# One of four channel blocks of a depthwise convolution goes from VectorE to GpSimd

## The chip, the cores and the metric

The kernel runs on one core of a Trainium2 chip, as one launch in float32. The metric is the device time of one execution in microseconds, the median of several runs. A core has TensorE (matmul, weight load), VectorE (elementwise and reductions), ScalarE (activation functions), GpSimd (elementwise, and DMAs with computed addresses) and SyncE (here only DMAs). They run side by side and wait for each other through semaphores. In the profile they are PE (and PEld), DVE, ACT, POOL and SP.

## The reference: what is computed

It is one inference step of a decoder layer for a prompt group of 1024 tokens and a sample group of 8. Three branches (latent attention, a convolution module, cross-attention to a memory) are gated, added, projected, and followed by a mixture of experts. The change lies in the convolution module. Its input is the gated product of 512 channels; `hist` puts 30 zero rows (prompt) or 30 state rows (sample) ahead of it. Each channel has its own 31 taps:

```python
y = lax.conv_general_dilated(hist, w_dw[:, None, :], window_strides=(1,), padding='VALID',
                             dimension_numbers=('NWC', 'WIO', 'NWC'), feature_group_count=C_CONV)
y = jax.nn.silu(layer_norm(y + b_dw, g_ln, b_ln))
return y @ w_conv_out
```

The layer norm is over the 512 channels, so its mean needs all of them. The merge is `(g_a * y_mla + g_b * y_conv + g_c * y_mem) @ w_out`.

## The kernel before, in words

The kernel is a chain of stages with a barrier between them: constants, front, tokens, sample, merge, mixer, experts. The change is in `stage_merge` alone, which runs from about 1121 to 1597 us of the profile. All engines' programs are written out by hand, each in a fixed order, with semaphores between them.

Channels lie on the partitions: 512 channels are KC = 4 blocks of 128, tokens run along the free dimension (SEQ = 1024, with the sample group TOK = 1032). The stage has three parts of KD = 8 blocks of output channels, a block has three units of 344 tokens, so there are 72 units u. Units 0 to 23 (up to U_C) take the attention branch, 24 to 47 (up to U_B) the memory branch, 48 to 71 the convolution branch.

- TensorE computes for a unit the gate (`pG`, 8 products in k, L1664; not for units 24 to 47, whose gates were stored earlier) and the branch (`pY`, 4 products in k, L1669). `pY` has two buffers: the branch of unit u waits for `unit_used` of u + 2, which is VectorE's merge of unit u - 2, and the gate of unit u for the merge of u - 3. In the profile each product appears as two passes (x8 is one unit's branch, x16 one unit's gate).
- ScalarE takes the sigmoid of the gate (L1561, or L1558 from stored gates). In units 0 to 3 it also takes the sigmoid of one block of convolution gates (L1564).
- VectorE merges the unit: L1617 for the first branch, L1621 and L1623 for the others. In units 0 to 3 it also writes one block of `hist` (L1607) and of `hist_s` (L1608), each marked on the semaphore `glu`.
- Behind the merge, VectorE runs a piece of the prompt's convolution, `conv(first, to)`: NTAP = 4 x 31 = 124 taps in order, four in unit 0, five a unit up to unit 23, three a unit after. A block's first tap is a `tensor_scalar` with the bias (L1593), the others are a `scalar_tensor_tensor` of 128x1024 that adds hist times tap to y (L1596), each waiting for the one before on the semaphore `tap`. After a block's last tap come three short operations for the sample group (L1599, L1601, L1603), marked on `conv_s`.
- In unit 23 VectorE also copies the last rows out of PSUM (L1635, L1636).
- After block b = KD (unit 26) TensorE waits for `conv_s` = 12 and `last_ready`, and adds y over the channels with a matrix of ones: `sums(y, 0)`, L1675 and L1677. The mean is used in units 27 to 30 (L1644), the squares (L1568) are summed after unit 32, the normalised values (L1652, L1576) are TensorE's input from unit 48 on.
- GpSimd clears three buffers and copies the sample group's attention outputs at the stage's start, and has nothing more to do in it.

Of the kernel before, what the change touches and what calls it, by code (L numbers as in the profile page):

```python
# [13 lines left out]
ALU = mybir.AluOpType  # L14
ACT = mybir.ActivationFunctionType
AX = mybir.AxisListType

P = 128
D = 1024
KD = D // P  # L20
SEQ = 1024
NT = SEQ // P
DB = 8
TOK = SEQ + DB
# [5 lines left out]
KC = CC // P  # L30
CW = 31
# [18 lines left out]
def spread(ap, n, at=1):  # L50

    v = ap.unsqueeze(at)
    shape = list(v.shape)
    shape[at] = n
    return v.broadcast_to(shape)
# [1387 lines left out]
def stage_merge(nc, a, o, keep):  # L1443
# [4 lines left out]
    U_C, U_B, U_END = 3 * KD, 6 * KD, 9 * KD  # L1448
    U_LAST, U_MEAN, U_VAR = U_C // 2, U_C + 3, U_C + 9
    PROMPT_END = SEQ - 2 * GN  # L1450
    NTAP = KC * CW
    with Core(nc) as c:
        ring = [c.sb(f"branch_w{r}", [P, 2 * KD, P]) for r in range(W)]
        gates = [ring[r][:, 4:2 * KD, :].rearrange("p k n -> p (k n)")[:, 0:TOK] for r in range(W)]
# [13 lines left out]
        mean = c.sb("ln_mean", [P, TOK])  # L1468
        state = mean[0:120, 0:2 * CC].rearrange("p (g c) -> p g c", g=2)
        ones = c.sb("ones", [P, P])  # L1470
        last = c.sb("last_rows", [HIST, CC])
        last_s = c.sb("last_rows_s", [DB, CC])
        eps = c.sb("eps", [P, 1])
# [3 lines left out]
        pX = c.ps("pSums")  # L1477
        pMs = pX[:, 0:2 * DB]
        S = {n: c.sem("m_" + n) for n in """small_in state_in cleared o_in o_sample unit_psum sig_ready unit_used gated taps_psum taps_ready
            state_psum state_ready glu_sig glu tap conv_s mean_psum mean_ready centred squares var_psum sqrt_ready recip normed conv_ready  # L1480
            last_psum last_ready stored state_moved""".split()}
        w_in = [c.sem(f"m_w_in{r}") for r in range(W)]
        raw_in = [c.sem(f"m_raw_in{i}") for i in range(KC)]
# [4 lines left out]
        with c.block() as block:  # L1488
# [43 lines left out]
            @block.gpsimd  # L1532
            def _(pool):
                pool.memset(ones[:, :], 1.0).then_inc(S["cleared"], 1)
                pool.memset(hist[:, :, 0:HIST], 0.0).then_inc(S["cleared"], 1)
                pool.memset(eps[:, :], EPS).then_inc(S["cleared"], 1)
                pool.tensor_copy(oT[:, 0, :, SEQ:TOK], keep.oT_s[:, :, :]).then_inc(S["o_sample"], 1)
                pool.tensor_copy(oT[:, 1, :, SEQ:TOK], keep.moT_s[:, :, :]).then_inc(S["o_sample"], 1)

            @block.scalar  # L1540
            def _(act):
# [37 lines left out]
            def _(v):  # L1579
# [3 lines left out]
                def conv(first, to):  # L1583

                    for n in range(first, min(to, NTAP)):
                        i, j = divmod(n, CW)
                        if n == 0:
                            v.wait_ge(S["small_in"], 64)
                            v.wait_ge(S["taps_ready"], 1)
                            v.wait_ge(S["state_ready"], 2)  # L1590
                        if j == 0:
                            v.wait_ge(S["glu"], 2 * i + 2)
                            v.tensor_scalar(y[:, i, 0:SEQ], hist[:, i, 0:SEQ], taps[:, i, 0:1], b_dw[:, i:i + 1], ALU.mult, ALU.add).then_inc(S["tap"], 1)  # L1593
                            continue
                        v.wait_ge(S["tap"], n)
                        v.scalar_tensor_tensor(y[:, i, 0:SEQ], hist[:, i, j:j + SEQ], taps[:, i, j:j + 1], y[:, i, 0:SEQ],  # L1596
                                               ALU.mult, ALU.add).then_inc(S["tap"], 1)
                        if j == CW - 1:
                            v.tensor_tensor(prod_s[:, :, :], hist_s[:, i, :, :], spread(taps[:, i, :], DB), ALU.mult).then_inc(S["conv_s"], 1)  # L1599
                            v.wait_ge(S["conv_s"], 3 * i + 1)  # L1600
                            v.tensor_reduce(y[:, i, SEQ:TOK], prod_s[:, :, :], AX.X, ALU.add).then_inc(S["conv_s"], 1)  # L1601
                            v.wait_ge(S["conv_s"], 3 * i + 2)
                            v.tensor_scalar(y[:, i, SEQ:TOK], y[:, i, SEQ:TOK], b_dw[:, i:i + 1], None, ALU.add).then_inc(S["conv_s"], 1)  # L1603

                def gated_unit(i):
                    v.wait_ge(S["glu_sig"], i + 1)
# [19 lines left out]
                for u in range(U_END):  # L1626
                    merge(u)
                    if u < KC:
                        gated_unit(u)
                    step = (4 if u == 0 else 5) if u < U_C else 3  # L1630
                    conv(done, done + step)
                    done += step
                    if u == U_C - 1:
                        v.wait_ge(S["last_psum"], 1)
                        v.tensor_copy(last[:, :], pM[0:HIST, 0:CC]).then_inc(S["last_ready"], 1)  # L1635
                        v.tensor_copy(last_s[:, :], pM[0:DB, CC:2 * CC]).then_inc(S["last_ready"], 1)  # L1636
                    if u == U_MEAN:
                        v.wait_ge(S["mean_psum"], 1)
                        v.tensor_scalar(mean[:, 0:SEQ], pM[:, :], -1.0 / CC, None, ALU.mult)
                        v.tensor_scalar(mean[:, SEQ:TOK], pMs[:, 0:DB], -1.0 / CC, None, ALU.mult).then_inc(S["mean_ready"], 1)  # L1640
                        v.wait_ge(S["mean_ready"], 1)
                    if U_MEAN <= u < U_MEAN + KC:
                        i = u - U_MEAN
                        v.tensor_tensor(y[:, i, :], y[:, i, :], mean[:, :], ALU.add).then_inc(S["centred"], 1)  # L1644
                    if U_VAR + 1 <= u < U_VAR + 4:
                        i = u - U_VAR - 1
                        v.wait_ge(S["sqrt_ready"], 1)
                        v.reciprocal(mean[:, i * GN:(i + 1) * GN], mean[:, i * GN:(i + 1) * GN]).then_inc(S["recip"], 1)
                    if U_VAR + 4 <= u < U_VAR + 4 + KC:
                        i = u - U_VAR - 4  # L1650
                        v.wait_ge(S["recip"], 3)
                        v.tensor_tensor(y[:, i, :], y[:, i, :], mean[:, :], ALU.mult).then_inc(S["normed"], 1)  # L1652

            @block.tensor
            def _(pe):
# [16 lines left out]
                def sums(src, col):  # L1672
                    for at in (0, 512):
                        for i in range(KC):
                            pe.matmul(pM[:, at:at + 512], ones[:, :], src[:, i, at:at + 512], start=i == 0, stop=i == KC - 1)  # L1675
                    for i in range(KC):
                        mm = pe.matmul(pMs[:, col:col + DB], ones[:, :], src[:, i, SEQ:TOK], start=i == 0, stop=i == KC - 1)  # L1677
                    return mm
# [24 lines left out]
                for b in range(KD, 2 * KD):  # L1703
                    block_of(b, oT[:, 1, :, :])
                    if b == KD:
                        pe.wait_ge(S["last_ready"], 2)
                        pe.wait_ge(S["conv_s"], 3 * KC)
                        sums(y, 0).then_inc(S["mean_psum"], 1)
                    if b == KD + 2:
                        pe.wait_ge(S["mean_ready"], 1)  # L1710
                        pe.wait_ge(S["squares"], KC)
                        sums(convT, DB).then_inc(S["var_psum"], 1)
# [714 lines left out]
```

## Time and profile before

| what | value |
| --- | --- |
| median of 3 runs | 3020.0 us (3019.23 to 3020.17) |
| profiled execution, its own time | 3025.34 us |
| span in the profile | 3023.6 us |
| mean granted TensorE clock | 0.949 of full speed |
| TensorE busy | 2775.9 us (92%) |
| VectorE busy | 1083.5 us (36%) |
| ScalarE busy | 621.3 us (21%) |
| GpSimd busy | 863.7 us (29%) |

The profile is of one execution. Its times count from its first instruction; its own time is 5.3 us above the median of the runs, and 1.7 us above its span. Busy shares are means over stages that differ much, so the merge stage has to be read by itself.

### The profile page before, as it was taken

Reading aid. Unit: us, or ns where it says so; the run is one execution under the profiler, and the core shown is the slowest. Engines: PE = TensorE matmul, PEld = TensorE weight load, DVE = VectorE, ACT = ScalarE, POOL = GpSimd, SP = SyncE. Lnnn points to the kernel's source line nnn. Section 1 sums busy time; section 2 is a strip of 40 time slices with the busy share of each in tenths; the row PEclk is TensorE's granted clock in tenths of the full one; section 3 lists DMA queues with packets and bytes.
Section 4 is the critical chain, followed back from the end, with each engine's and each line's share of the span. In section 5 each row is a group of like instructions: output and inputs, shape, how many; then the busy total and the mean of one; then the engine's idle time right before and its main releaser. Section 6 shows DMA issues by size and latency. Waiting matters only on the chain. (4 is left out here: it accounts for less than half of the span.)

```text
span 3023.6 us, 34530 instructions
## 1 busy us (share of the span) xinstructions
PE 2775.9 (92%) x12222; PEld 1854.5 (61%) x12222; DVE 1083.5 (36%) x2253; ACT 621.3 (21%) x1186; POOL 863.7 (29%) x680
## 2 busy tenths in 40 slices
PE   6999999998999976989996998489999999999996
PEld 4566666655555544655663444277777777777774
DVE  3233444453333324995111443322222222222221
ACT  2233333332333311004000110011111111111111
POOL 1000000000544420000000222255555555555552
PEclk9999999997999977989997988789999999999998
DMA  7111110103322114112104111189999999999995
GB/s 252 37 42 47 40 38 26 33 20 84 101 74 81 46 41 141 37 42 75 32 11 159 42 59 39 59 293 303 292 297 295 301 293 298 295 300 294 299 295 147
DMA packets 212823, 428.02 MB, mean 142 GB/s; under 512 B 52898, under 2 KB 134580, under 8 KB 196249
## 3 DMA queue, kind: packets, MB, share of 16 engines
q1 hardware_dynamic: 164592, 316.35, 30.7%
q0 software_dynamic: 35168, 100.78, 13.2%
q10 hardware_dynamic: 12960, 9.58, 1.0%
q8 instruction: 58, 0.95, 0.1%
q14 instruction: 45, 0.36, 0.0%
HBM read 351.23 MB, written 80.68 MB: 143 GB/s over the span
## 5 line engine op out<-in xcount | busy, mean ns | idle before, releaser
L2162 POOL DMA_INDIRECT xg<-tokens_normed,gather_rows x384 | 369.1, 961 | 132.3 <-issue 117.3
L2297 PE MATMUL pGe<-xT,we_g 128*128 128x192 f32 x2048 | 352.7, 331 | 45.1 <-DVE xT L2249 45.1
L2297 PEld LDWEIGHTS pGe<-xT,we_g 128*128 128x128 f32 x2048 | 334.0, 191 | 96.2 <-issue 96.2
L2297 PE MATMUL pUe<-xT,we_u 128*128 128x192 f32 x2048 | 343.3, 326 | 0.0
L2297 PEld LDWEIGHTS pUe<-xT,we_u 128*128 128x128 f32 x2048 | 334.6, 190 | 0.0
L2185 POOL DMA_INDIRECT sums<-yb,add_rows x128 | 195.9, 1531 | 352.4 <-ACT yb L2213 307.2
L1318 PE MATMUL pKs<-ws_uk,cTs 128*128 128x512 f32 x512 | 254.2, 642 | 1.1 <-ACT cTs L1105 1.1
L805 PE MATMUL pFill<-hT,fill_w 128*128 128x344 f32 x768 | 239.5, 456 | 7.1 <-ACT fill_out L514 7.0
L1664 PE MATMUL pGate<-hT,branch_w 128*128 128x344 f32 x768 | 232.1, 455 | 10.9 <-DMA oT<-attention_out 10.9
L1083 POOL TENSOR_TENSOR rk<-ssk,half 128x32 f32<-128x32 f32 x32 | 173.4, 5427 | 216.0 <-DVE ssk L1187 216.0
L2307 PE MATMUL pYe<-we_d,h_e 128*128 128x512 f32 x512 | 230.3, 592 | 0.0
L1664 PEld LDWEIGHTS pGate<-hT,branch_w 128*128 128x128 f32 x768 | 146.9, 191 | 88.0 <-DMA oT<-attention_out 11.3
L2249 DVE STREAM_TRANSPOSE xT<-xg 128x1536 f32<-128x1536 f32 x64 | 189.4, 2959 | 20.5 <-DMA xg<-tokens_normed,gather_rows 20.5
L805 PEld LDWEIGHTS pFill<-hT,fill_w 128*128 128x128 f32 x768 | 141.7, 190 | 83.6 <-issue 21.8
L2255 DVE TENSOR_TENSOR h_e<-silu,pUe 128x384 f32<-128x384 f32 x64 | 35.5, 554 | 435.3 <-PE pUe L2297 435.3
L2213 ACT ACTIVATE yb<-pYe,wc 128x512 f32<-128x512 f32 x128 | 87.9, 687 | 472.1 <-PE pYe L2307 472.1
L1244 DVE TENSOR_REDUCE ssk<-sqs 128x8 f32<-128x512 f32 x128 | 87.6, 684 | 237.8 <-ACT sqs L1131 237.4
L1318 PEld LDWEIGHTS pKs<-ws_uk,cTs 128*128 128x128 f32 x512 | 99.3, 205 | 104.2 <-issue 101.2
L1596 DVE SCALAR_TENSOR_TENSOR y_conv<-hist,taps,y_conv 128x1024 f32<-128x1024 f32 x120 | 154.0, 1284 | 3.4
L2280 DVE TENSOR_SCALAR yb<-pZe,wc 64x512 f32<-64x512 f32 x64 | 47.5, 743 | 300.1 <-PE pZe L2313 300.1
L2307 PEld LDWEIGHTS pYe<-we_d,h_e 128*128 128x128 f32 x512 | 95.5, 190 | 92.7 <-issue 92.7
L2020 PE MATMUL pXf<-w_out,mT 128*128 128x512 f32 x288 | 127.1, 600 | 15.0 <-DMA w_out<-in_w_out 15.0
(387 smaller groups left out, 3201.9 us busy)
## 6 DMA issues: line engine op xcount, KB each, us to landing
we_g<-in_w_e_gate SPq DMA_DIRECT2D x64, 1024.0 KB, 5.2
we_u<-in_w_e_up SPq DMA_DIRECT2D x64, 1024.0 KB, 9.6
we_d<-in_w_e_down SPq DMA_DIRECT2D x64, 1024.0 KB, 14.6
mergedT<-in_cache_latent SPq DMA_DIRECT2D x96, 128.0 KB, 2.1
raw_columns<-fill_out SPq DMA_DIRECT2D x48, 172.0 KB
fill_w<-in_w_in SPq DMA_DIRECT2D x16, 512.0 KB, 4.3
branch_w<-in_w_in SPq DMA_DIRECT2D x16, 512.0 KB, 4.3
xg<-tokens_normed,gather_rows POOLq DMA_INDIRECT x384
```

Source lines behind the costliest of these rows:

```text
L805: mm = pe.matmul(pG[:, 0:GN], ring[b % 2][:, k, :], keep.hT[:, k, g * GN:(g + 1) * GN], start=k == 0, stop=k == KD - 1)
L1083: pool.tensor_tensor(rk[b % 2][:, :, g, :], ssk[b % 2][:, :, g, :], half[:, :].rearrange("p (j h) -> p j h", h=NHEAD), ALU.pow).then_inc(S ...
L1318: mm = pe.matmul(pK[n % 2][:, :], cT[b % 2][:, k, n * P:(n + 1) * P], w_uk[:, k, :], start=k == 0, stop=k == KL - 1)
L1596: v.scalar_tensor_tensor(y[:, i, 0:SEQ], hist[:, i, j:j + SEQ], taps[:, i, j:j + 1], y[:, i, 0:SEQ], ALU.mult, ALU.add).then_inc(S["tap"], 1)
L1664: pe.matmul(pG[g][:, 0:n], ring[r][:, 4 + k, :], keep.hT[:, k, at:at + n], start=k == 0, stop=k == KD - 1)
L2020: mm = pe.matmul(pX[:, half * 512:(half + 1) * 512], mT[:, k, :], w_out[:, k, half * 512:(half + 1) * 512], start=k == 0, stop=k == KD - 1)
L2162: pool.indirect_dma_start(out=xg[s % 2][:, g, :], out_offset=None, in_=quarter, in_offset=bass.IndirectOffsetOnAxis(ap=gi[s][:, g:g + 1], ...
L2185: pool.indirect_dma_start(out=keep.acc_dram[:, :], out_offset=bass.IndirectOffsetOnAxis(ap=si[r][0:n_of[g], g:g + 1], axis=0), in_=yb[r % ...
L2213: act.activation(yb[r % 2][:, 0, half * 512:(half + 1) * 512], pY[half][:, :], ACT.Copy, scale=wc[r][:, 0:1]).then_inc(S["y_act"], 1)
L2249: v.transpose(xT[p][:, :, :].rearrange("p c (g i) -> p g c i", g=NG_E), xg[p][:, :, :].rearrange("p g (j c) -> p g c j", c=KD)).then_inc(S ...
L2297: mm = pe.matmul(dst[r % 2][:, f * CAP:(f + 1) * CAP], w[r][:, k, f * P:(f + 1) * P], xT[r % 2][:, k, :], start=k == 0, stop=k == KD - 1)
L2307: mm = pe.matmul(pY[half][:, :], h[r % 2][:, f, 0:P], wd[r][:, f, half * 512:(half + 1) * 512], start=f == 0, stop=f == 1)
```

## The change

The fourth block of channels (KV = 3) of the prompt's convolution is computed on GpSimd, the first three stay on VectorE. VectorE's NTAP becomes 93, four taps in each of units 0 to 23 (the last has one), none after. GpSimd waits until all four blocks of `hist` are written (`glu` = 8) and runs the first tap with the bias as before; for each of the other 30 taps it writes the product into the new buffer `one_tap` and adds that to y, and each of these waits for the one before (`pool_tap`, `pool_mult`). The sample group's three short operations become a function, `conv_sample(i)`; all four blocks of it stay on VectorE, the fourth in unit 23. TensorE's sums and VectorE's subtraction of the mean also wait for `pool_tap` = 31.

```diff
--- before.py
+++ after.py
@@ -1448,7 +1448,8 @@
     U_C, U_B, U_END = 3 * KD, 6 * KD, 9 * KD
     U_LAST, U_MEAN, U_VAR = U_C // 2, U_C + 3, U_C + 9
     PROMPT_END = SEQ - 2 * GN
-    NTAP = KC * CW
+    KV = KC - 1
+    NTAP = KV * CW
     with Core(nc) as c:
         ring = [c.sb(f"branch_w{r}", [P, 2 * KD, P]) for r in range(W)]
         gates = [ring[r][:, 4:2 * KD, :].rearrange("p k n -> p (k n)")[:, 0:TOK] for r in range(W)]
@@ -1468,6 +1469,7 @@
         mean = c.sb("ln_mean", [P, TOK])
         state = mean[0:120, 0:2 * CC].rearrange("p (g c) -> p g c", g=2)
         ones = c.sb("ones", [P, P])
+        one_tap = c.sb("one_tap", [P, SEQ])
         last = c.sb("last_rows", [HIST, CC])
         last_s = c.sb("last_rows_s", [DB, CC])
         eps = c.sb("eps", [P, 1])
@@ -1477,7 +1479,7 @@
         pX = c.ps("pSums")
         pMs = pX[:, 0:2 * DB]
         S = {n: c.sem("m_" + n) for n in """small_in state_in cleared o_in o_sample unit_psum sig_ready unit_used gated taps_psum taps_ready
-            state_psum state_ready glu_sig glu tap conv_s mean_psum mean_ready centred squares var_psum sqrt_ready recip normed conv_ready
+            state_psum state_ready glu_sig glu tap pool_tap pool_mult conv_s mean_psum mean_ready centred squares var_psum sqrt_ready recip normed conv_ready
             last_psum last_ready stored state_moved""".split()}
         w_in = [c.sem(f"m_w_in{r}") for r in range(W)]
         raw_in = [c.sem(f"m_raw_in{i}") for i in range(KC)]
@@ -1536,6 +1538,16 @@
                 pool.memset(eps[:, :], EPS).then_inc(S["cleared"], 1)
                 pool.tensor_copy(oT[:, 0, :, SEQ:TOK], keep.oT_s[:, :, :]).then_inc(S["o_sample"], 1)
                 pool.tensor_copy(oT[:, 1, :, SEQ:TOK], keep.moT_s[:, :, :]).then_inc(S["o_sample"], 1)
+                pool.wait_ge(S["small_in"], 64)
+                pool.wait_ge(S["taps_ready"], 1)
+                pool.wait_ge(S["glu"], 2 * KC)
+                rows = y[:, KV, 0:SEQ]
+                pool.tensor_scalar(rows, hist[:, KV, 0:SEQ], taps[:, KV, 0:1], b_dw[:, KV:KC], ALU.mult, ALU.add).then_inc(S["pool_tap"], 1)
+                for j in range(1, CW):
+                    pool.wait_ge(S["pool_tap"], j)
+                    pool.tensor_scalar(one_tap[:, :], hist[:, KV, j:j + SEQ], taps[:, KV, j:j + 1], None, ALU.mult).then_inc(S["pool_mult"], 1)
+                    pool.wait_ge(S["pool_mult"], j)
+                    pool.tensor_tensor(rows, rows, one_tap[:, :], ALU.add).then_inc(S["pool_tap"], 1)
 
             @block.scalar
             def _(act):
@@ -1596,11 +1608,16 @@
                         v.scalar_tensor_tensor(y[:, i, 0:SEQ], hist[:, i, j:j + SEQ], taps[:, i, j:j + 1], y[:, i, 0:SEQ],
                                                ALU.mult, ALU.add).then_inc(S["tap"], 1)
                         if j == CW - 1:
-                            v.tensor_tensor(prod_s[:, :, :], hist_s[:, i, :, :], spread(taps[:, i, :], DB), ALU.mult).then_inc(S["conv_s"], 1)
-                            v.wait_ge(S["conv_s"], 3 * i + 1)
-                            v.tensor_reduce(y[:, i, SEQ:TOK], prod_s[:, :, :], AX.X, ALU.add).then_inc(S["conv_s"], 1)
-                            v.wait_ge(S["conv_s"], 3 * i + 2)
-                            v.tensor_scalar(y[:, i, SEQ:TOK], y[:, i, SEQ:TOK], b_dw[:, i:i + 1], None, ALU.add).then_inc(S["conv_s"], 1)
+                            conv_sample(i)
+
+                def conv_sample(i):
+                    v.wait_ge(S["state_ready"], 2)
+                    v.wait_ge(S["glu"], 2 * i + 2)
+                    v.tensor_tensor(prod_s[:, :, :], hist_s[:, i, :, :], spread(taps[:, i, :], DB), ALU.mult).then_inc(S["conv_s"], 1)
+                    v.wait_ge(S["conv_s"], 3 * i + 1)
+                    v.tensor_reduce(y[:, i, SEQ:TOK], prod_s[:, :, :], AX.X, ALU.add).then_inc(S["conv_s"], 1)
+                    v.wait_ge(S["conv_s"], 3 * i + 2)
+                    v.tensor_scalar(y[:, i, SEQ:TOK], y[:, i, SEQ:TOK], b_dw[:, i:i + 1], None, ALU.add).then_inc(S["conv_s"], 1)
 
                 def gated_unit(i):
                     v.wait_ge(S["glu_sig"], i + 1)
@@ -1627,10 +1644,11 @@
                     merge(u)
                     if u < KC:
                         gated_unit(u)
-                    step = (4 if u == 0 else 5) if u < U_C else 3
+                    step = 4 if u < U_C else 0
                     conv(done, done + step)
                     done += step
                     if u == U_C - 1:
+                        conv_sample(KV)
                         v.wait_ge(S["last_psum"], 1)
                         v.tensor_copy(last[:, :], pM[0:HIST, 0:CC]).then_inc(S["last_ready"], 1)
                         v.tensor_copy(last_s[:, :], pM[0:DB, CC:2 * CC]).then_inc(S["last_ready"], 1)
@@ -1641,6 +1659,7 @@
                         v.wait_ge(S["mean_ready"], 1)
                     if U_MEAN <= u < U_MEAN + KC:
                         i = u - U_MEAN
+                        v.wait_ge(S["pool_tap"], CW)
                         v.tensor_tensor(y[:, i, :], y[:, i, :], mean[:, :], ALU.add).then_inc(S["centred"], 1)
                     if U_VAR + 1 <= u < U_VAR + 4:
                         i = u - U_VAR - 1
@@ -1705,6 +1724,7 @@
                     if b == KD:
                         pe.wait_ge(S["last_ready"], 2)
                         pe.wait_ge(S["conv_s"], 3 * KC)
+                        pe.wait_ge(S["pool_tap"], CW)
                         sums(y, 0).then_inc(S["mean_psum"], 1)
                     if b == KD + 2:
                         pe.wait_ge(S["mean_ready"], 1)
```

## Rows read from the trace of the kernel before

**Rows 1.** The page, part 1: busy time, share of the span, instructions.

```profile
PE 2775.9 (92%) x12222; PEld 1854.5 (61%) x12222; DVE 1083.5 (36%) x2253; ACT 621.3 (21%) x1186; POOL 863.7 (29%) x680
```

**Rows 2.** Busy time by stretch: window, its length, busy (instructions), then clock, DMA, GB/s.

```profile
core 0: us, PE busy (x) PEld busy (x) DVE busy (x) ACT busy (x) POOL busy (x), PEclk, DMA share, GB/s
...
1195.00:1332.00 137.00, 137.00 (x481) 90.07 (x480) 134.14 (x129) 8.69 (x19) 0.00 (x0) 1.00 0.11 35
1332.00:1354.00 22.00, 11.67 (x25) 6.14 (x23) 21.50 (x25) 2.68 (x6) 0.00 (x0) 0.70 0.21 71
1354.00:1364.00 10.00, 9.97 (x26) 4.96 (x27) 0.86 (x2) 0.00 (x0) 0.00 (x0) 0.81 0.00 2
```

**Rows 3.** Timeline from 1165 us: start, length, engine, line, operation, out<-in, count.

```profile
1192.29 4.79 PE L1664 MATMUL pGate<-hT,branch_w 128*128 128x344 f32 x16
...
1195.87 0.51 DVE L1617 TENSOR_TENSOR mergedT<-gate_sig,pBranch 128x344 f32<-128x344 f32 x1
...
1197.42 0.17 DVE L1608 TENSOR_TENSOR hist_s<-convT,y_conv 128x8 f32<-128x8 f32 x1
...
1199.23 4.79 PE L1664 MATMUL pGate<-hT,branch_w 128*128 128x344 f32 x16
```

**Rows 4.** Instructions that write or read y_conv: durations ns min/median/max, first and last start.

```profile
L1596 DVE SCALAR_TENSOR_TENSOR y_conv<-hist,taps,y_conv x120: 1276/1285/1286, 1175.4 to 1351.6; 128x1024 f32<-128x1024 f32 x120
...
L1607 DVE TENSOR_TENSOR hist<-convT,y_conv x4: 1220/1222/1226, 1173.1 to 1196.3; 128x1024 f32<-128x1024 f32 x4
...
L1593 DVE TENSOR_SCALAR y_conv<-hist,taps,b_dw x4: 806/809/812, 1174.6 to 1308.1; 128x1024 f32<-128x1024 f32 x4
```

**Rows 5.** Timeline from unit 23 to the second sums, in order of start.

```profile
1329.65 4.79 PE L1669 MATMUL pBranch<-oT,branch_w 128*128 128x344 f32 x16
...
1336.38 0.51 DVE L1617 TENSOR_TENSOR mergedT<-gate_sig,pBranch 128x344 f32<-128x344 f32 x1
1336.81 6.56 DVE L1596 SCALAR_TENSOR_TENSOR y_conv<-hist,taps,y_conv 128x1024 f32<-128x1024 f32 x5
...
1336.94 4.27 PE L1669 MATMUL pBranch<-oT,branch_w 128*128 128x344 f32 x8 [2.50 <-DVE mergedT L1617]
...
1343.29 0.67 DVE L1635 COPY last_rows<-pM 30x512 f32<-30x512 f32 x1
...
1345.03 4.96 PE L1669 MATMUL pBranch<-oT,branch_w 128*128 128x344 f32 x8 [3.81 <-DVE gated L1621]
...
1352.77 0.41 DVE L1599 TENSOR_TENSOR prod_s<-hist_s,taps 128x248 f32<-128x248 f32 x1
...
1354.03 8.93 PE L1675 MATMUL pM<-y_conv,ones 128*128 128x512 f32 x16 [4.05 <-DVE y_conv L1603]
...
1363.60 14.13 PE L1669 MATMUL pBranch<-oT,branch_w 128*128 128x344 f32 x48
...
1377.57 7.03 PE L1675 MATMUL pM<-convT,ones 128*128 128x512 f32 x16
...
1385.24 10.08 PE L1669 MATMUL pBranch<-oT,branch_w 128*128 128x344 f32 x34
```

**Rows 6.** GpSimd's groups by line: count | busy us, mean ns | idle before, releaser.

```profile
L1083 POOL TENSOR_TENSOR rk<-ssk,half 128x32 f32<-128x32 f32 x32 | 173.4, 5427 | 216.0 <-DVE ssk L1187 216.0
...
L1832 POOL MEMSET zero<- 128x1024 f32 x1 | 1.0, 952 | 0.0
...
L1071 POOL MEMSET q_a<- 128x512 f32 x1 | 0.5, 528 | 0.0
```

**Rows 7.** Timeline of GpSimd and of VectorE in the sample stage.

```profile
870.17 10.82 POOL L1083 TENSOR_TENSOR rk<-ssk,half 128x32 f32<-128x32 f32 x2 [12.80 <-DVE ssk L1187]
...
874.79 0.19 DVE L1187 SCALAR_TENSOR_TENSOR ssk<-ssk,sskr 128x32 f32<-128x32 f32 x1
...
877.11 0.29 DVE L1219 TENSOR_TENSOR s_keys<-s_keys,mb 128x128 f32<-128x128 f32 x1
```

**Rows 8.** The instructions of line L1219: durations ns min/median/max.

```profile
L1219 DVE TENSOR_TENSOR s_keys<-s_keys,mb x8: 291/293/293, 786.1 to 1102.4; 128x128 f32<-128x128 f32 x8
```

## The prediction

> **What bounds the kernel now.** The page comes first: TensorE is busy 92% of the span [rows 1], so the first question for any edit is whether TensorE waits for the edited work. The change sits in the merge stage, so the second view is the table of busy time by stretch of that stage [rows 2]. From 1195 to 1332 us TensorE is busy 137.00 of 137.00 us and VectorE 134.14. VectorE is nearly as full, but not what sets the pace: TensorE's units follow each other at 1199.23 - 1192.29 = 6.94 us [rows 3]. From 1332 to 1354 us TensorE is busy only 11.67 of 22 us, while VectorE is busy 21.50. That stretch is what the change can win. The timeline says what happens there [rows 5]: unit 23's merge on VectorE comes at 1336.38, behind five taps of unit 22. It is followed by five more taps, the copies of the last rows at 1343.29, and the last five taps; the all-ones sums over the channels start only at 1354.03, when the last convolution value is written. TensorE waits three times, and its granted clock falls to a mean of 0.70 of full speed [rows 2], between its levels 2.4 and 1.2 GHz. The first sums, begun in that state, take 1363.60 - 1354.03 = 9.57 us, the second, after busy matmuls, 1385.24 - 1377.57 = 7.67 us [rows 5].
>
> **What goes away.** VectorE drops 31 of 124 taps: 30 of 1.285 us and one of 0.81 us [rows 4], 39.3 us. Start to start a tap takes 6.56 / 5 = 1.31 us [rows 5]. A plain unit then has four taps and a merge, 5.25 + 0.51 = 5.8 us, against TensorE's 6.94; the first four units also make the gated rows (1.22 + 0.17 us, the latter for the sample group [rows 3, 4]): 7.1 us, a backlog of 0.6 us in all, soon gone.
>
> The end of the branch, if GpSimd costs nothing: TensorE finishes units 23 and 24 at 1329.65 + 4.79 = 1334.4 [rows 5]. VectorE, no longer behind, merges unit 23 from about 1332.7 (half of those 4.79 us, then ScalarE's sigmoid) to 1333.2. It has one tap left (93 - 92), then two sample convolutions instead of one (three short operations, from 1352.77 to the sums at 1354.03, 1.2 us each), then the two copies, 1.3 us: 1333.2 + 1.3 + 2.4 + 1.3 = 1338.2. Its merge of unit 24 releases TensorE's unit 26 at 1338.7. That takes 2.5 us (half the 4.79 of two), so the sums start at 1341.2 instead of 1354.0: 12.8 us sooner. They also run at the full clock: 9.57 - 7.67 = 1.9 us. Together **-14.7 us**. What follows (mean, squares, normalising) keeps its order and lengths, so it shifts as a whole.
>
> **What GpSimd is given.** It starts when the fourth gated rows are written. Unit 3's merge was at 1195.87 [rows 3]; two taps fewer by then put it at 1193.3, and the merge and the two gated-row operations end at about 1195.2. It has one first tap, 30 products and 30 sums of 128x1024, each waiting for the one before. No row of before shows such an operation. Near rows: MEMSET takes 0.952 us for 1024 columns and 0.528 for 512 [rows 6], 0.83 ns a column, one write each. A one-operand product is at least that, 0.95, and at most a read and a write in turn, 0.95 + 0.85 = 1.80. A sum reads two operands: 1.80 at least, 2.65 if the write comes in turn too. I take 1.1 and 2.2: reads in turn, writes mostly beside them. 31 x 1.1 + 30 x 2.2 = 100, with 0.05 us from each to the next 103 us; the ends are 84 + 3 and 135 + 3. The pow row (5.4 us for 32 columns [rows 6]) is work of another kind and no bound. The chain alone ends at 1298, at worst at 1333, and the sums could not start before 1341. By its own length GpSimd is hidden; it would decide from 146 us on, or 4.8 us for a product and sum.
>
> **What both do to each other.** For those 103 us VectorE runs a tap with two SBUF operands 5.25 of every 6.94 us. The question is whether such a tap and a streaming GpSimd operation read side by side. The trace tests it only weakly [rows 7]: while GpSimd is in two pows (870.17 to 880.99), VectorE's two-operand operations at 874.79 and 877.11 take 0.19 and 0.29 us and start without delay; the second has 291 to 293 ns in all eight cases [rows 8]. So a GpSimd instruction does not shut VectorE out for its whole length. But a pow needs 64 values a partition in 5.4 us, which is 64 x 0.83 ns = 0.05 us of reading: 1% of its time. The new operations read nearly throughout. The lower bound of the interference is therefore nothing, the upper bound strict turns. I take turns, as the reading of both is almost uninterrupted.
>
> Turns: 61 GpSimd operations each let one tap through, so both together take 61 x 1.31 + 103 = 183 us, to 1378. VectorE's merges hide behind GpSimd's operations; a unit takes 4 x 1.31 + 4 x 1.69 = 12.0 us in place of 6.94, and as TensorE has only two buffers of branch results, it slows with VectorE. At 1378 VectorE has done 12 + 61 = 73 taps. The 20 left and five merges take 26.2 + 2.6 = 28.8, the tail after unit 23's last tap 2.4 + 1.3 + 0.5 = 4.2, TensorE's unit 26 2.5: sums at 1413.7. That is 59.7 us later than 1354.0, less 1.9 for the clock: **+57.8 us**. Against the profiled execution's 3025.3 us this gives 3083.1; the median of the runs is 5.3 lower: **3078 us**. If VectorE goes first always and GpSimd gets only the 1.7 us that a unit leaves, it has 21 x 1.7 = 36 of 103 us done by 1341, and the sums start at 1408: 3072, so the order of turns hardly matters. Ends by GpSimd's two lengths: 87 us gives 3062, 138 us gives 3113. If TensorE's clock fell in the half-idle units (58% busy; at 0.53 busy it was 0.70 [rows 2]) to its lower level, eight matmuls would take about 4.3 us for 2.48 (the 1336.94 row [rows 5]), and a unit of 24 some 13 us, more than the 12.0: up to 15 us more.
>
> The Trainium skill ("SBUF — State Buffer", Who interferes with whom) says that a VectorE instruction with two SBUF inputs contends with a GpSimd instruction that reads SBUF, and that the second to issue blocks fully until the first is done. By that rule the sum is the turns above; by the pow rows, which do not show a block for the whole instruction, it would be -14.7 us.
>
> **Rivals.**
> 1. Side by side, nothing lost: the -14.7 us stand, 3005 us. For it: the undelayed operations of [rows 7, 8]. Against: they say little of streams. It ends on the other side, and decides as long as a product and sum stay under 4.8 us and the taps near 1.3.
> 2. A finer sharing: reads mix element by element on one path. GpSimd needs 91 operand streams (1 + 30 + 60) of 1024 x 0.83 ns = 0.85 us, 77 us; VectorE's taps 79 x 1.28 = 101 us. Together 178 us from 1195.2: sums at 1373, 19.2 - 1.9 = +17.3: 3037 us; less, if the taps need the path for only part of their time.
> 3. GpSimd long by itself: at over 4.8 us a pair (a pow costs 170 ns a column, [rows 6]) the sums wait for GpSimd with VectorE idle; each 1 us a pair adds 30 us. At 6 us: 1195 + 1 + 180 = 1376, 3040 us. Nothing in the MEMSET rows speaks for it.
>
> **How the numbers follow.** Turns 0.50 (3062 to 3113), side by side 0.30 (3002 to 3010), finer sharing 0.14 (3018 to 3050), long GpSimd 0.06. A difference of 0.2%, 6 us, is about what a measurement of this kernel can tell from none. Faster: the side by side case and a little of the sharing, 0.33. Within 6 us: 0.07. Slower: 0.60. The range has to hold both main cases: 3003 to 3108; the likeliest case's own is 3062 to 3113.
>
> **What would show it.** The profile after should have GpSimd busy over 31 TENSOR_SCALAR and 30 TENSOR_TENSOR from about 1195. Turns: taps in the 1195 to 1378 stretch start 2.4 to 4 us apart or last that long, units 12 us apart, pGate waiting for merges, sums at about 1413. Side by side: taps stay at 1.28 us, units at 6.94, GpSimd ends near 1298, sums at 1341. Sharing: both kinds of operation longer than alone, and no strict alternation. The forecast is wrong if the taps keep their 1.28 us beside GpSimd's stream; the size is wrong if GpSimd's pair is not 3.3 us.

## The result and the profile after

The kernel after takes 3058.8 us (median of 4 runs, 3055.6 to 3059.2), before 3019.7; the ratio is 1.0127, 95% interval 1.0110 to 1.0145. It is 39 us slower, within the stated range of 3003 to 3108. It is 3 us below the 3062 to 3113 that turns alone were to give, and above the 3018 to 3050 of a finer sharing. Of the 12 executions of e11, further down, one ran at a granted clock of 0.78 and took 5373 us; it is left out of that run's median.

The profiled execution took 3055.55 us. The stages ahead of the merge stage, the same code in both, ran 8.0 us shorter in it than in the profile of before, so times are best counted from the stage's own start, GpSimd's first MEMSET in it (1121.47 us before, 1113.47 after). To the first MEMSET of the next stage it is 475.8 us before and 517.5 after: **+41.7 us**; the medians give 39.1. TensorE's sums over the channels start 232.6 us into the stage before and 273.9 after: +41.3 us. So nearly all of it arises ahead of the sums, in the stretch that the prediction spoke of.

The page of the kernel after, part 1, against [rows 1]:

```profile
PE 2776.4 (91%) x12222; PEld 1851.1 (61%) x12222; DVE 1116.7 (37%) x2222; ACT 621.7 (20%) x1186; POOL 1060.0 (35%) x741
```

TensorE does the same work. VectorE is busy 33 us longer although it has 31 taps fewer. GpSimd has 196 us more, for a chain forecast at 103. By stretch (window, length, busy by engine with instructions, clock, DMA, GB/s), against [rows 2]:

```profile
core 0: us, PE busy (x) PEld busy (x) DVE busy (x) ACT busy (x) POOL busy (x), PEclk, DMA share, GB/s
...
1195.00:1250.00 55.00, 50.20 (x172) 32.13 (x170) 54.33 (x32) 3.20 (x7) 53.45 (x18) 1.00 0.15 43
...
1332.00:1354.00 22.00, 17.00 (x56) 10.39 (x56) 21.72 (x15) 1.30 (x4) 21.37 (x8) 1.00 0.00 1
...
1364.00:1400.00 36.00, 22.76 (x52) 11.80 (x52) 16.19 (x21) 1.47 (x3) 22.57 (x8) 0.67 0.07 22
```

In the first branch TensorE was busy 137 of 137 us; now it is 50.2 of 55 and 17.0 of 22, and VectorE and GpSimd are both full. In the last stretch it has 22.8 of 36 at a granted clock of 0.67. The instructions that write or read y_conv (durations ns min/median/max, first and last start), against [rows 4], show what VectorE is full of:

```profile
L1608 DVE SCALAR_TENSOR_TENSOR y_conv<-hist,taps,y_conv x90: 1269/2020/3260, 1167.5 to 1367.9; 128x1024 f32<-128x1024 f32 x90
L1550 POOL TENSOR_TENSOR y_conv<-y_conv,one_tap x30: 2338/2789/3094, 1193.4 to 1384.9; 128x1024 f32<-128x1024 f32 x30
```

A tap took 1276 to 1286 ns before; now 1.27 to 3.26 us, median 2.02. GpSimd's groups (count, busy us, mean ns, idle before), which have no counterpart before:

```profile
L1548 POOL TENSOR_SCALAR one_tap<-hist,taps 128x1024 f32<-128x1024 f32 x30 | 108.5, 3618 | 2.9
L1550 POOL TENSOR_TENSOR y_conv<-y_conv,one_tap 128x1024 f32<-128x1024 f32 x30 | 83.6, 2788 | 2.5
...
L1545 POOL TENSOR_SCALAR y_conv<-hist,taps,b_dw 128x1024 f32<-128x1024 f32 x1 | 2.0, 2024 | 73.4 <-DVE hist_s L1625 73.4
```

A product of the chain costs 3.6 us, a sum 2.8. The timeline of the end of the chain, against [rows 5]:

```profile
1366.93 2.79 POOL L1550 TENSOR_TENSOR y_conv<-y_conv,one_tap 128x1024 f32<-128x1024 f32 x1
1367.43 0.51 DVE L1634 TENSOR_TENSOR mergedT<-gate_sig,pBranch 128x344 f32<-128x344 f32 x1
1367.85 2.95 DVE L1608 SCALAR_TENSOR_TENSOR y_conv<-hist,taps,y_conv 128x1024 f32<-128x1024 f32 x1
...
1373.84 2.34 POOL L1550 TENSOR_TENSOR y_conv<-y_conv,one_tap 128x1024 f32<-128x1024 f32 x1
1374.19 0.49 DVE L1638 TENSOR_TENSOR gated<-gate_sig,pBranch 128x344 f32<-128x344 f32 x1
1374.72 1.84 DVE L1640 TENSOR_TENSOR mergedT<-mergedT,gated 128x344 f32<-128x344 f32 x1
...
1384.86 2.34 POOL L1550 TENSOR_TENSOR y_conv<-y_conv,one_tap 128x1024 f32<-128x1024 f32 x1
...
1387.34 8.83 PE L1694 MATMUL pM<-y_conv,ones 128*128 128x512 f32 x16 [7.66 <-POOL y_conv L1550]
...
1396.83 5.45 PE L1688 MATMUL pBranch<-oT,branch_w 128*128 128x344 f32 x18
```

Three things are to be seen here. The tap of 1367.85 begins beside GpSimd's sum, which ends at 1369.72, and lasts until 1370.80: the sum's end and 1.08 us more. The same happens to the merge's addition of two SBUF operands at 1374.72, 1.84 us for 0.52, held until the sum of 1373.84 is over at 1376.18; the merge's product at 1374.19, with one operand in PSUM, lies beside the same sum and takes its usual 0.49. And the last to finish is GpSimd, at 1387.20, 16 us after VectorE's last tap. TensorE's waits in this stage (in total, times, longest us):

```profile
PE pBranch L1688 <- DVE mergedT L1634: 31.4, 13, 6.2
...
PE pM L1694 <- POOL y_conv L1550: 7.7, 1, 7.7
```

Thirteen times a unit waits for a merge that is late behind taps; once, TensorE's sums wait for GpSimd. Before, a merge had kept a unit of the first branch waiting only at its very end [rows 5].

### The profile page after: what moved, and what is told of

Read it like the earlier page. It is cut to its first block and busy times, and to the rows that moved or that the text cites. A ratio compares the mean times of both kernels' runs of the same rounds, so it can differ in the third digit from the quotient of the medians.

```text
span 3053.6 us, 34568 instructions
## 1 busy us (share of the span) xinstructions
PE 2776.4 (91%) x12222; PEld 1851.1 (61%) x12222; DVE 1116.7 (37%) x2222; ACT 621.7 (20%) x1186; POOL 1060.0 (35%) x741
## 5 line engine op out<-in xcount | busy, mean ns | idle before, releaser
L1083 POOL TENSOR_TENSOR rk<-ssk,half 128x32 f32<-128x32 f32 x32 | 173.4, 5428 | 211.5 <-DVE ssk L1187 211.5
L1608 DVE SCALAR_TENSOR_TENSOR y_conv<-hist,taps,y_conv 128x1024 f32<-128x1024 f32 x90 | 180.7, 2008 | 2.4
L1688 PE MATMUL pBranch<-oT,branch_w 128*128 128x344 f32 x384 | 130.5, 492 | 39.6 <-DVE mergedT L1634 31.4
```

Source lines behind the costliest of these rows:

```text
L1083: pool.tensor_tensor(rk[b % 2][:, :, g, :], ssk[b % 2][:, :, g, :], half[:, :].rearrange("p (j h) -> p j h", h=NHEAD), ALU.pow).then_inc(S ...
L1688: mm = pe.matmul(pY[u % 2][:, 0:n], ring[r][:, k, :], branch[:, k, at:at + n], start=k == 0, stop=k == 3)
```

## The experiments

For each run: when TensorE's sums over the channels start and how long the stage is, both in us and from the same MEMSETs; the mean length of VectorE's taps; the median of GpSimd's products and sums; the device time.

| run | sums start | stage | tap | product | sum | time |
| --- | --- | --- | --- | --- | --- | --- |
| before | 232.6 | 475.8 | 1.28 | | | 3020 |
| after | 273.9 | 517.5 | 2.01 | 3.70 | 2.79 | 3058.8 |
| e1 GpSimd alone | 237.1 | 482.0 | | 2.84 | 2.35 | (4070.6) |
| e2 VectorE alone | 219.0 | 460.4 | 1.29 | | | (4048.1) |
| e3 products only | 219.0 | 460.3 | 1.50 | 3.28 | | (4050.5) |
| e4 sums only | 257.6 | 498.9 | 1.88 | | 3.21 | (4082.4) |
| e5 addend in PSUM | 237.9 | 482.4 | 1.28 | 2.84 | 2.36 | (4065.8) |
| e6 writes only | 219.0 | 460.8 | 1.29 | | | (4046.9) |
| e7 products on ScalarE | 251.3 | 493.1 | 1.90 | | 3.03 | 3035.4 |
| e9 two-scalar product | 273.2 | 515.0 | 2.11 | 2.05 | 3.19 | 3053.8 |
| e12 taps in PSUM, plain product | 237.1 | 481.9 | 1.29 | 2.84 | 2.35 | 3025.1 |
| e10 taps in PSUM | 218.1 | 459.9 | 1.29 | 1.20 | 2.35 | 2999.5 |
| e11 before, sums later | 236.1 | 470.5 | 1.28 | | | 3010.3 |

Times in brackets are of kernels that leave out or change part of the convolution. Their tokens are routed differently and the experts' stage makes two passes for one (4096 products into pGe for 2048), some 1043 us more from the first of these to the end. They are compared by the stage alone; e2, e3, e4 and e6, which compute the same, also with each other.

### GpSimd alone, VectorE alone

The first theory: each engine is held up while the other reads SBUF over a path that both need. The rival: GpSimd is just slow. Run e1:

```diff
-                        v.wait_ge(S["tap"], n)
-                        v.scalar_tensor_tensor(y[:, i, 0:SEQ], hist[:, i, j:j + SEQ], taps[:, i, j:j + 1], y[:, i, 0:SEQ],
-                                               ALU.mult, ALU.add).then_inc(S["tap"], 1)
```

> Left out: the 90 scalar_tensor_tensor taps of VectorE, so that GpSimd works on its block alone. Reading theory (each engine is held up while the other reads SBUF over a path that both need): GpSimd's operations fall to what they take in the kernel after once VectorE is done, product 2.98 us, sum 2.34 us, 5.5 us for the pair with gaps; the chain takes 2 + 30 x 5.5 = 167 us instead of 200, and TensorE's first sums wait for it, so that the merge stage is some 8 us longer than before. Rival (GpSimd is only slow, VectorE has nothing to do with it): product 3.70, sum 2.79, chain 200 us, as in the kernel after, and the merge stage about 40 us longer than before.

The instructions on one_tap in this run:

```profile
L1548 POOL TENSOR_SCALAR one_tap<-hist,taps x30: 2842/2842/2983, 1190.8 to 1347.4; 128x1024 f32<-128x1024 f32 x30
L1550 POOL TENSOR_TENSOR y_conv<-y_conv,one_tap x30: 2337/2346/2672, 1193.7 to 1350.3; 128x1024 f32<-128x1024 f32 x30
```

As the theory has it: 2.84 and 2.35 us, against 3.70 and 2.79 with VectorE's taps (medians). But the rival has its part too: by itself the chain lasts 163.1 us, from 73.9 to 237.0, and TensorE's sums already wait for it, 4.5 us later than in the kernel before. The first tap of the chain, a multiply and an add with two scalars, takes 1.19 us, less than half of a plain product. That was not expected and is followed up below. Run e2:

```diff
-                for j in range(1, CW):
-                    ... (GpSimd's product and sum)
+                pool.sem_inc(S["pool_tap"], CW - 1)
```

> Left out: GpSimd's 30 products and 30 sums, so that block 3 has its first tap only. Reading theory: the taps are back at 1.28 us, units follow at 6.94 us, TensorE's sums start 12.8 us sooner than before, some 3005 us, the gain that the edit would have brought if GpSimd cost nothing. Rival (VectorE is not slowed by GpSimd's work but by something else of the new program): taps stay near 2 us.

```profile
L1604 DVE SCALAR_TENSOR_TENSOR y_conv<-hist,taps,y_conv x90: 1276/1285/2104, 1172.2 to 1329.9; 128x1024 f32<-128x1024 f32 x90
```

The taps are back at 1285 ns (one of them meets GpSimd's first tap, 2104 ns). The sums start 13.6 us sooner than before, the stage is 15.4 us shorter; 12.8 and 14.7 were forecast.

### Which of GpSimd's operations holds VectorE up

Run e3:

```diff
-                    pool.tensor_scalar(one_tap[:, :], ..., None, ALU.mult).then_inc(S["pool_mult"], 1)
-                    pool.wait_ge(S["pool_mult"], j)
-                    pool.tensor_tensor(rows, rows, one_tap[:, :], ALU.add).then_inc(S["pool_tap"], 1)
+                    pool.tensor_scalar(one_tap[:, :], ..., None, ALU.mult).then_inc(S["pool_tap"], 1)
```

> Left out: GpSimd's 30 sums; the products stay, each behind the one before. Reading theory: a product holds a tap up by 0.74 us (2.02 - 1.28 in the kernel after), and GpSimd needs 3.1 to 3.8 us for each; 30 x 0.74 = 22 us of delay within some 100 us, most of it in VectorE's slack of 1.1 us a unit; the time is about 3010 us. Rival (GpSimd holds its path for an instruction's whole length): a tap waits up to 3 us for each product, 30 x 3 = 90 us of delay, less 20 of slack: some 3070 us. Rival (length of GpSimd's chain is all): 3005 us.

Groups of this run (count, busy us, mean ns, idle before):

```profile
L1606 DVE SCALAR_TENSOR_TENSOR y_conv<-hist,taps,y_conv 128x1024 f32<-128x1024 f32 x90 | 135.1, 1501 | 2.4
...
L1548 POOL TENSOR_SCALAR one_tap<-hist,taps 128x1024 f32<-128x1024 f32 x30 | 99.7, 3324 | 2.8
```

Products do hold taps up, 90 x (1.50 - 1.28) = 20 us in all, 0.7 us for each product, and VectorE's slack takes it: the sums start at 219.0 as without them. A product of 2.84 us does not shut VectorE out for its length; that rival falls. Run e4:

```diff
+                pool.memset(one_tap[:, :], 0.0).then_inc(S["pool_mult"], 1)
+                pool.wait_ge(S["pool_mult"], 1)
-                    pool.tensor_scalar(one_tap[:, :], ..., None, ALU.mult).then_inc(S["pool_mult"], 1)
-                    pool.wait_ge(S["pool_mult"], j)
```

> Left out: GpSimd's 30 products; the sums stay (they add a buffer of zeros), each behind the one before. Reading theory: a sum reads nearly all its time and holds a tap up by 1.98 us (3.26 - 1.28); taps and sums take turns at some 3.35 us for both, a unit of four taps takes 13 us while the 30 sums last, 100 us, 7.6 units: about 46 us of delay, 3050 us. Rival (length of the chain is all): 30 x 2.4 = 72 us, hidden, 3005 us.

```profile
L1608 DVE SCALAR_TENSOR_TENSOR y_conv<-hist,taps,y_conv 128x1024 f32<-128x1024 f32 x90 | 169.3, 1881 | 2.4
...
L1550 POOL TENSOR_TENSOR y_conv<-y_conv,one_tap 128x1024 f32<-128x1024 f32 x30 | 94.2, 3142 | 2.4
```

GpSimd's sums alone cost 257.6 - 219.0 = 38.6 us, most of the 273.9 - 219.0 = 54.9 us between e2 and the kernel after, by 90 x (1.88 - 1.28) = 54 us of longer taps. 46 was forecast. The chain ends at 173.4. Behind it VectorE merges a unit every 5.6 us until it has caught up with TensorE, and from then on every 6.9 us, TensorE's own pace: the time that TensorE lost beside the chain stays lost.

### What exactly collides

Run e5:

```diff
-                        v.scalar_tensor_tensor(y[:, i, 0:SEQ], hist[...], taps[:, i, j:j + 1], y[:, i, 0:SEQ], ALU.mult, ALU.add)
+                        v.scalar_tensor_tensor(y[...], hist[...], taps[:, i, j:j + 1], spread(pX[:, :], 2), ALU.mult, ALU.add)
```

> Changed: VectorE's taps take their addend from PSUM (a bank of zeros) and not from y, so that only one of their operands lies in SBUF; the convolution of the three blocks comes out wrong. GpSimd's chain is that of the kernel after. Reading theory in its narrow form (VectorE's second SBUF operand comes over the path that GpSimd reads by): taps keep their own length beside GpSimd's work, GpSimd's product and sum take 2.84 and 2.35 us as in the run without taps, and TensorE's sums start 237 us after the stage's start, against 274 in the kernel after. Rival (any reading by both engines collides): taps still last 2.0 to 3.3 us beside GpSimd, sums at 260 us or later.

```profile
L1610 DVE SCALAR_TENSOR_TENSOR y_conv<-hist,taps,pSums x90: 1272/1281/1282, 1166.7 to 1324.5; 128x1024 f32<-128x1024 f32 x90
L1550 POOL TENSOR_TENSOR y_conv<-y_conv,one_tap x30: 2337/2357/2682, 1191.0 to 1348.3; 128x1024 f32<-128x1024 f32 x30
```

With one operand in PSUM every one of the 90 taps takes 1272 to 1282 ns beside GpSimd's full chain, and GpSimd's operations have the median lengths that they have alone. For the taps, the collision is that of two inputs in SBUF with GpSimd's chain; whether it is with its reading, e6 tells:

```diff
-                    (product)
+                    pool.memset(one_tap[:, :], 1.0).then_inc(S["pool_mult"], 1)
-                    (sum)
+                    pool.memset(one_tap[:, :], 0.0).then_inc(S["pool_tap"], 1)
```

> Changed: GpSimd's 30 products and 30 sums are replaced by 60 MEMSETs of the same buffer size, each behind the one before; block 3 has its first tap only. Reading theory: nothing is read by GpSimd, so taps stay at 1.28 us and the sums start at 219 us after the stage's start, as with GpSimd's chain left out. Rival (GpSimd's writes collide with VectorE's too, or its instructions as such do): taps are held up, by about 0.9 us for each MEMSET, sums at 240 us or later.

```profile
L1608 DVE SCALAR_TENSOR_TENSOR y_conv<-hist,taps,y_conv x90: 1277/1285/2105, 1166.7 to 1324.4; 128x1024 f32<-128x1024 f32 x90
```

60 MEMSETs of 0.95 us leave the taps alone (the one of 2105 ns meets GpSimd's first tap, which reads), so for them it is GpSimd's reading that counts. Its writing is not free for all that VectorE does. In the same run, us from start:

```profile
1217.08 0.95 POOL L1548 MEMSET one_tap<- 128x1024 f32 x1
1217.21 0.84 DVE L1620 TENSOR_SCALAR y_conv<-y_conv,b_dw 128x8 f32<-128x8 f32 x1
1217.35 1.23 DVE L1605 TENSOR_SCALAR y_conv<-hist,taps,b_dw 128x1024 f32<-128x1024 f32 x1
1218.09 1.39 POOL L1550 MEMSET one_tap<- 128x1024 f32 x1
```

VectorE's small TENSOR_SCALAR, with one input and the output in SBUF, takes 0.84 us for 0.23 and ends with the MEMSET beside it. The next MEMSET, beside the large one, takes 1.39 us for 0.95. The kernel has only a handful of such instructions, so this costs next to nothing here.

### Less reading, and a shorter chain

Run e7:

```diff
+                            act.wait_ge(S["pool_tap"], j - 1)
+                            act.activation(one_tap[:, j % 2, :], hist[:, KV, j:j + SEQ], ACT.Copy, scale=taps[:, KV, j:j + 1]).then_inc(S["pool_mult"], 1)
-                    pool.tensor_scalar(one_tap[:, :], hist[:, KV, j:j + SEQ], taps[:, KV, j:j + 1], None, ALU.mult)...
```

> Changed: ScalarE makes the 30 products (three in two units, from unit 4 on, two buffers); GpSimd only adds; all of the computation is done. Reading theory: the products' 0.74 us each go, the sums' 1.98 us stay. VectorE's work from 74 us after the stage's start: 81 taps x 1.31 + 30 x 1.98 + some 10 for merges and the sample group, so TensorE's sums start at about 250 to 254 us, against 274 after and 233 before: 3038 us, faster than the kernel after and still slower than before. Rival (GpSimd's own length is what costs): the chain ends by 200 us and the time is 3005 us.

```profile
L1613 DVE SCALAR_TENSOR_TENSOR y_conv<-hist,taps,y_conv x90: 1271/1285/3267, 1168.2 to 1358.0; 128x1024 f32<-128x1024 f32 x90
L1549 POOL TENSOR_TENSOR y_conv<-y_conv,one_tap x30: 2347/3033/3397, 1193.9 to 1350.7; 128x1024 f32<-128x1024 f32 x30
```

3035.4 us, ratio to before 1.0053 (1.0032 to 1.0074), the sums at 251.3: as forecast, better than the change and still a loss. A sum costs VectorE 1.98 us and saves it a tap of 1.31. Run e9:

```diff
-                    pool.tensor_scalar(one_tap[:, :], hist[...], taps[:, KV, j:j + 1], None, ALU.mult)
+                    pool.tensor_scalar(one_tap[:, :], hist[...], taps[:, KV, j:j + 1], hist[:, KV, 0:1], ALU.mult, ALU.add)
```

> Changed: GpSimd's product becomes multiply by the tap and add a zero taken from hist's padding, the form of its first tap, which took 1.19 us without VectorE's taps where the plain product took 2.84; all of the computation is done. Reading theory: GpSimd's chain gets shorter by up to 30 x 1.65 us, but each product and sum still holds VectorE up by 0.74 and 1.98 us, so VectorE's end stays at about 260 us after the stage's start, and only the 14 us by which GpSimd ended later than VectorE are won: 3045 to 3048 us. Rival (the two-scalar form is no faster, the first tap was quick for another reason): 3059 us as the kernel after. Rival (GpSimd's length is all): 3005 us.

```profile
L1548 POOL TENSOR_SCALAR one_tap<-hist,taps x30: 1241/2048/2054, 1194.2 to 1349.4; 128x1024 f32<-128x1024 f32 x30
L1550 POOL TENSOR_TENSOR y_conv<-y_conv,one_tap x30: 2845/3192/3199, 1196.4 to 1351.5; 128x1024 f32<-128x1024 f32 x30
```

The two-scalar product is quick (1.24 us where no tap is in its way), and the chain ends at 236.5 for 273.7. But the sums start at 273.2, and 3053.8 us (ratio 1.0108, 1.0084 to 1.0132) miss the 3045 to 3048. What the expectation left out: now every product and sum falls beside taps, while in the kernel after the last three of each came when VectorE was done with them. So the 90 taps take 190.1 us in all for 180.7, and the last of them ends at 267.1 for 257.3. VectorE, a unit every 5.6 us behind the chain, is what ends last, and the sums follow 6.1 us after its last tap.

### Keeping the taps out of the way

If two SBUF operands collide, VectorE's sums can be kept in PSUM. Only a block's last tap writes y; the last rows' transposes go to the bank of the small sums (that part of the edit isn't shown). Run e12:

```diff
-                            v.tensor_scalar(y[:, i, 0:SEQ], hist[:, i, 0:SEQ], ...)
+                            v.wait_ge(S["tap"], n)
+                            v.tensor_scalar(pM[:, :], hist[:, i, 0:SEQ], ...)
-                        v.scalar_tensor_tensor(y[:, i, 0:SEQ], hist[...], taps[:, i, j:j + 1], y[:, i, 0:SEQ], ...)
+                        v.scalar_tensor_tensor(y[:, i, 0:SEQ] if j == CW - 1 else pM[:, :], hist[...], taps[:, i, j:j + 1], pM[:, :], ...)
```

> As the kernel with taps in PSUM, but with GpSimd's product in its plain form. Reading theory: taps at 1.28 us, GpSimd's pair 2.84 + 2.35 + 0.2 = 5.4 us, its chain ends at 74 + 2 + 162 = 238 us after the stage's start and sets the sums' start, 5 us later than before: about 3025 us. Rival (the length of GpSimd's chain does not count once VectorE is free): 3005 us.

The wait in question (in total, times, longest us):

```profile
PE pM L1698 <- POOL y_conv L1550: 15.1, 1, 15.1
```

3025.1 us, ratio 1.0015 (1.0007 to 1.0024): even without a collision the change does not pay, because the chain, 163 us long, ends at 237 and TensorE waits 15.1 us for it. 3025 was forecast.

Run e10 has the same taps and e9's product:

> Changed against the kernel after: VectorE's three blocks accumulate in PSUM (two banks), only a block's last tap writes y; the last rows' transposes move to the sums' bank for it; GpSimd's product has the two-scalar form. All of the computation is done. Reading theory: a tap then has one operand in SBUF and stays at 1.28 us beside GpSimd's work; GpSimd's pair takes 1.2 + 2.4 + 0.2 = 3.8 us, its chain ends 74 + 115 = 189 us after the stage's start, hidden; TensorE's sums start at 219 us as with GpSimd's chain left out, and the time is 14 to 15 us below before, 3005 us: the gain that the change was after. Rival (PSUM operands are no cure, or writing to PSUM makes a tap longer than 1.35 us): sums at 225 us or later, or taps of 2 us again.

```profile
L1609 DVE SCALAR_TENSOR_TENSOR pM<-hist,taps,pM x87: 1275/1290/1291, 1170.7 to 1324.8; 128x1024 f32<-128x1024 f32 x87
```

```profile
L1548 POOL TENSOR_SCALAR one_tap<-hist,taps x30: 1194/1195/1237, 1191.4 to 1299.8; 128x1024 f32<-128x1024 f32 x30
L1550 POOL TENSOR_TENSOR y_conv<-y_conv,one_tap x30: 2344/2352/2383, 1192.7 to 1301.0; 128x1024 f32<-128x1024 f32 x30
```

```profile
1331.64 2.58 PE L1692 MATMUL pBranch<-oT,branch_w 128*128 128x344 f32 x8 [0.26 <-DVE gated L1639]
...
1334.06 7.03 PE L1698 MATMUL pM<-y_conv,ones 128*128 128x512 f32 x16
```

With the quick product too the chain ends at 187.4 and nothing waits for it: TensorE goes from unit 26's branch at 1331.64 to the sums at 1334.06, where it had three waits before [rows 5], and the 16 large products of the sums take 7.03 us, at the full clock, for 8.93. The time is 2999.5 us (median of 6), ratio 0.9936 (0.9923 to 0.9949): 19.6 us faster than the 3019.0 of before in the same series, and a stage 15.9 us shorter, where 14 to 15 were forecast. This is the gain that the change was after. It needs both edits: with e9's product alone the time is 3053.8 us, with the taps in PSUM alone 3025.1.

Run e11, made from the kernel before:

```diff
-    U_LAST, U_MEAN, U_VAR = U_C // 2, U_C + 3, U_C + 9
+    U_LAST, U_MEAN, U_VAR = U_C // 2, U_C + 6, U_C + 12
-                    step = (4 if u == 0 else 5) if u < U_C else 3
+                    step = (4 if u == 0 else 5) if u < U_C else 2
-                    if b == KD:
+                    if b == KD + 1:
-                    if b == KD + 2:
+                    if b == KD + 3:
```

> Made from the kernel before, with no work on GpSimd: TensorE's sums, the mean and all that hangs on it come one block (three units) later, and from unit 24 on VectorE has two taps a unit, so that TensorE works on the memory branch while VectorE ends the taps. Waiting theory (the 22 us at the end of the first branch, of which TensorE worked 12, are all that the change could win, and part of it can be had without GpSimd): three units of 2.5 us fill the wait, VectorE's merges between its taps take 3 us of it back: 3 to 6 us below before, 3015 us. Rival (TensorE's units then wait for VectorE's merges instead): no change.

3010.3 us, ratio 0.9976 (0.9965 to 0.9987), which is 7 to 9 us below before, and the stage is 5.3 us shorter; 3 to 6 were forecast. So part of the wait can be had with VectorE alone.

## Why the prediction came out as it did

The direction and the cause (taps and GpSimd's operations take turns) were right, their strictness and the lengths were not: +57.8 us in the forecast, +41.7 in the stage and +39.1 by the medians.

- **What could be won.** Right. With GpSimd out of it the stage is 15.4 us shorter (e2), 14.7 were forecast.
- **GpSimd's start.** Right: 74.1 us into the stage, 73.7 forecast (1195.2 - 1121.5).
- **The lengths.** GpSimd's sum was taken at 2.2 us and takes 2.35 alone. The product was taken at 1.1, with 1.80 as the upper end, and takes 2.84 alone. MEMSET's pace was no guide to the one-scalar form. The chain alone is 163 us, not 103, and outside the bounds of 87 to 138. So the rival of a long GpSimd, given 0.06, holds as well: at 5.4 us for a pair it is past the 4.8 from which GpSimd decides, and the sign that the prediction named for a wrong size, a pair other than 3.3 us, is there.
- **Turns.** Nearly right for the sum: it holds a tap up for 1.98 of its 2.35 us, 3.26 us for 1.28. Wrong for the product: of its 2.84 us it keeps VectorE out for 0.74 (e3). The pows of [rows 7] had shown no delay, and with 1% of reading could not. So three taps, not two, pass with a product and a sum: 2.02 + 1.28 + 3.26 and the gaps are the 6.66 us from product to product (1196.33, 1202.99 in the trace). Between the merges of units 4 and 23 (1193.93 and 1367.43) a unit takes 173.5 / 19 = 9.1 us, where 12.0 stood in the forecast.
- **Who ends last.** The forecast had VectorE last. It was GpSimd: TensorE's unit 26 ends at 1379.69, TensorE's sums start at 1387.34, 7.7 us later. TensorE's clock was low again there, and they took 1396.83 - 1387.34 = 9.5 us, so the 1.9 us for the clock were not won.

The 41.3 us are thus: -13.6 for the shift of the taps (219.0 - 232.6), +47.2 for the slower units, the last of them at a low clock (unit 26 ends 266.2 us into the stage, against the 219.0 at which the sums start in e2), +7.7 for the wait for GpSimd. The forecast's +59.7 came from a slowdown that was too strong on a chain that was too short; the two errors cancelled in part, and that is luck. With the measured 163 us for the chain, strict turns would have given 61 x 1.31 + 163 = 243 us for the 183, and 3138 us. The forecast's kernel exists nearly as e9, with a product of about the forecast length. There a product and a sum take 5.43 us and two taps pass, where the forecast had 6.0; the chain takes 162.6 us for 183, and the sums start at 273.2 for 292.2 (1413.7 - 1121.5). So even with the right lengths the turns were some 19 us too strict, and the longer product of the kernel after, which lets taps through, costs hardly more (273.9).

The rule of the Trainium skill ("SBUF — State Buffer", Who interferes with whom, and the summary that ends the page) that the second to issue blocks fully until the first is done nearly agrees with the trace for the sum, and not for the product, which lets taps through for most of its 2.84 us. That a tap with one SBUF input stays out of it, and one with two stays out beside GpSimd instructions that only write, agrees (e5, e6).

What stays open: why a plain product takes 2.84 us and one with an added zero 1.20 us. The runs show that it is the form of the instruction (the buffers are the same but for a column of zeros), not why. Open too is whether VectorE's output counts: no run has both inputs in SBUF and the output in PSUM.

## What to carry to other kernels

Before elementwise work goes to GpSimd beside VectorE, look at where VectorE's operands lie: here an addition or a tap with both inputs in SBUF paid for GpSimd's reading, and one with an input in PSUM did not. A tap moved to GpSimd saved VectorE 1.31 us and cost it 2.7, so by these numbers no smaller share would have paid either, though no run has one; with the addend in PSUM it cost the taps nothing. And measure the length of each GpSimd instruction in the form in which it will run, for a form that looks like less work may take twice as long. Where one engine paces another through a small ring, time that the second loses in one stretch need not come back in the next: in e4 VectorE catches up behind the chain, and TensorE stays late.

## What was not expected of the hardware

- GpSimd's TENSOR_SCALAR of 128x1024 float32 takes 2.84 us with one scalar and one operation, and 1.20 us with two (e1, e10).
- A product of 2.84 us holds a two-operand tap up for 0.74 us, a sum of 2.35 us for 1.98 us, and a two-scalar product of 1.20 us for 0.82 us (e9: taps of 2.10 us for 1.28). So the quick product keeps VectorE out as long as the slow one. The other way round a tap makes a product 0.4 to 0.9 us longer and a sum 0.4 to 0.9 us.
- VectorE's small TENSOR_SCALAR from SBUF to SBUF (128x8, 0.23 us before) takes 0.44 to 2.30 us beside GpSimd's chain, and 0.84 us beside a MEMSET (e6), though it has one input; the one of 128x1024 stayed at 0.80 us in its two cases beside the chain of the kernel after.
- A tap that reads its addend from PSUM and writes PSUM takes 1.288 us, against 1.284 in SBUF. A block's first tap, a TENSOR_SCALAR, takes 1.33 to 1.35 us when it writes PSUM (e10), against 0.81 in SBUF.
